# A hand-written state-space stage: who stores u, in which order it lies in memory, and where the modulation products stand

## The reference, cut to what matters

```python
shift, scale, gate = _modulation(c, a_mod_w, a_mod_b, 3)      # silu(c) @ w + b
h = _rms(x, a_norm_g) * (1.0 + scale) + shift                 # x: 1024 tokens x 1024
u, z = jnp.split(h @ w_in, 2, axis=-1)                        # each 1024 x 1024
ug = u.reshape(bsz, L, N_GROUPS, GROUP)                       # 64 groups of 16 channels
bu_r = jnp.einsum('blgc,gpc->blgp', ug, bb_r)                 # and bu_i
_, _, s_r, s_i = lax.associative_scan(_cplx_combine, (a_r, a_i, bu_r, bu_i), axis=1)
y = (jnp.einsum('blgp,gcp->blgc', s_r, C_re) - jnp.einsum('blgp,gcp->blgc', s_i, C_im))
y = gelu(y.reshape(bsz, L, 1024) + D * u)
# then glu, times silu(z), times w_out, gate, residual; four more such modulations in later stages
```

## Time and profile before

| | us |
|---|---|
| median of three runs | 4381.43 |
| profiled execution, its own time | 4385.33 |
| its span | 4383.5 |
| TensorE busy in the span | 4061.4 (93%) |
| VectorE / ScalarE / GpSimd busy | 2700.2 / 1218.4 / 382.8 |

### The profile page before, as it was taken

How to read it: one execution, slowest core, us unless ns; L and a number is a source line. 1 busy time by engine, 2 the same in 40 slices (tenths; PEclk the granted TensorE clock), 3 DMA queues, 4 the chain that set the end, 5 groups by cost and what they waited for, 6 DMA issues and landing times. The chain is left out here.

```text
span 4383.5 us, 74028 instructions
## 1 busy us (share of the span) xinstructions
PE 4061.4 (93%) x29536; PEld 2617.4 (60%) x29536; DVE 2700.2 (62%) x5234; ACT 1218.4 (28%) x2794; POOL 382.8 (9%) x313
## 2 busy tenths in 40 slices
PE   7969999999998999998799999989989995899998
PEld 4434856888666788665444444448847774444443
DVE  6427334433576544755777887854436555899997
ACT  2111222212575322833211111122125642222112
POOL 0100000000121000000211111110000000212221
PEclk8989999999999999998899999999989997999999
DMA  7697211132431212105777777750153104799997
GB/s 285 235 192 270 83 72 40 66 109 86 155 117 59 85 53 91 48 31 199 273 263 293 284 273 271 271 196 20 52 179 87 21 31 164 277 353 348 349 349 288
DMA packets 138205, 757.96 MB, mean 173 GB/s; under 512 B 14848, under 2 KB 53504, under 8 KB 102512
## 3 DMA queue, kind: packets, MB, share of 16 engines
q1 hardware_dynamic: 108048, 670.05, 41.1%
q0 software_dynamic: 24880, 65.29, 5.7%
q10 hardware_dynamic: 5040, 19.37, 1.3%
HBM read 663.98 MB, written 91.19 MB: 172 GB/s over the span
## 5 line engine op out<-in xcount | busy, mean ns | idle before, releaser
L442 PE MATMUL psum<-w_ring,arena 128*128 128x256 f32 (+1 forms) x2784 | 611.3, 378 | 19.1 <-PEq L202 8.3
L442 PEld LDWEIGHTS psum<-w_ring,arena 128*128 128x128 f32 x2784 | 523.1, 192 | 90.9 <-issue 20.5
L3442 PE MATMUL psum<-arena 128*64 128x512 f32 x2048 | 454.7, 596 | 6.6 <-ACT arena L3631 4.5
L3464 PE MATMUL psum<-arena 128*64 128x256 f32 x3472 | 381.5, 380 | 0.0
L442 PE MATMUL psum<-arena,w_ring 128*128 128x256 f32 x1600 | 354.6, 381 | 6.4 <-DVE arena L497 3.5
L3442 PE MATMUL psum<-w_ring,arena 128*64 128x512 f32 x1536 | 344.3, 597 | 5.2 <-ACT arena L3764 5.2
L442 PEld LDWEIGHTS psum<-arena,w_ring 128*128 128x128 f32 x1600 | 303.0, 191 | 50.1 <-DVE w_ring L538 3.6
L3464 PEld LDWEIGHTS psum<-arena 128*64 128x64 f32 x3472 | 246.6, 137 | 122.9
L3442 PEld LDWEIGHTS psum<-arena 128*64 128x64 f32 x2048 | 147.5, 137 | 281.4 <-issue 280.4
L1863 PE MATMUL psum<-arena 48*128 48x512 f32 (+5 forms) x1440 | 292.4, 517 | 8.8 <-PEq L1476 3.5
L508 DVE TENSOR_TENSOR arena<-arena,psum 128x256 f32<-128x256 f32 (+1 forms) x92 | 38.5, 418 | 386.2 <-PE psum L442 386.1
(11 more groups left out here) (464 smaller groups left out, 6006.9 us busy)
## 6 DMA issues: line engine op xcount, KB each, us to landing
w_ring<-in_wstream SPq DMA_DIRECT2D x162, 2048.0 KB, 9.3
arena<-in_wstream SPq DMA_DIRECT2D x97, 2048.0 KB, 7.8
x_rows<-arena SPq DMA_DIRECT2D x26, 512.0 KB, 2.8
w_ring<-in_wstream ACTq DMA_DIRECT2D x6, 2048.0 KB, 8.0
arena<-x_rows SPq DMA_DIRECT2D x18, 512.0 KB, 7.1
xn_rows<-arena POOLq DMA_DIRECT2D x18, 512.0 KB, 7.2
arena<-f_rows SPq DMA_DIRECT2D x8, 1024.0 KB, 7.7
arena<-in_x_first SPq DMA_DIRECT2D x4, 1024.0 KB, 25.0
```

The lines of the kernel that those rows point to most:

```text
L442: last = self.cr.nc.tensor.matmul(out, l, r, start=(start and k == 0), stop=(k == len(pairs) - 1), skip_group_check=True)
L3442: last = nc.tensor.matmul(cr.bank[bank][HT * h:HT * (h + 1), :], left[:, k], right[:, 4 * h + k, :], start=(start and k == 0), stop=(k == ...
L3464: last = nc.tensor.matmul(cr.bank[bank][HT * h:HT * (h + 1), 0:QW], left[:, k], right[:, k, QW * h:QW * (h + 1)], start=(start and k == 0) ...
```

## The change

1. `u_T` in DRAM is laid out as [8 positions, 16 channels, 64 groups, 128 chunks]. Transfer t of the U load is then one run of 32 KB for each of 16 partitions, where it was 64 pieces of 512 B for each.
2. ScalarE stores u itself, on its own DMA queue: after the copy of u product p it waits for that copy and issues eight transfers, each from 16 partitions, four pieces of 512 B from each. GpSimd stores only z. The semaphores `ut` count these transfers in the place of `st`.
3. The scan inputs stand after products 18 and 19 (they stood after 20 and 21), and the sixteen modulation products are spaced by a table: none after 18, two after 26. The slots change with them: tile `W_AIN + 3` comes earlier in slot 1, and m = 2 to 7 all use slot 2. SyncE's extra load that waits for product 23 stands before the load that follows m = 6 (it stood before the one that follows m = 7).

```diff
-FIRST_SLOTS.update({W_MOD1 + n: 1 if n % 2 else 2 for n in range(6)})
-FIRST_SLOTS.update({W_AIN + 3: 1})
-FIRST_SLOTS.update({W_MOD1 + n: 0 if n > 8 and n % 2 else 2 for n in range(6, N_MOD1)})
+FIRST_SLOTS.update({W_MOD1: 2, W_MOD1 + 1: 1, W_AIN + 3: 1})
+FIRST_SLOTS.update({W_MOD1 + n: 0 if n >= 8 and n % 2 == 0 else 2 for n in range(2, N_MOD1)})
...
-    uT, zT = cr.dram("u_T", [D, SEQ]), cr.dram("z_T", [D, SEQ])
+    uT, zT = cr.dram("u_T", [T_CH, GRP, GROUPS, NCH]), cr.dram("z_T", [D, SEQ])
...
-    K_AT, G_AT, IN_AT = 8, 12, 20
-    mods_after = lambda p: range(p - 16, p - 15 if p < 30 else N_MOD1) if 16 <= p < 31 else ()
+    K_AT, G_AT, IN_AT = 8, 12, 18
+    MODS_AFTER = {16: (0,), 17: (1,), 19: (2,), 20: (3,), 21: (4,), 22: (5,), 23: (6,), 24: (7,), 25: (8,), 26: (9, 10), 27: (11,), 28: (12,), 29: (13,), 30: (14, 15)}
...
+    def emptied(eng, u):
+        if u < 16:
+            eng.wait_ge(ut[u % 2], 128 * (u // 2))
+        elif u == 16:
+            eng.wait_ge(ut[1], 128 * 8)
+        else:
+            eng.wait_ge(st[1], 16 * (u - 16))
...
             for s in range(2):
-                sp.wait_ge(st[s], 16 * NU // 4)
+                sp.wait_ge(ut[s], 128 * 8)
             sp.wait_ge(s_gt, 16)
             for t in range(T_CH):
-                sp.dma_start(U[GRP * t:GRP * (t + 1)], uT.rearrange("(g c) t -> c g t", c=GRP)[:, :, t * NCH:(t + 1) * NCH]).then_inc(u_in, 16)
+                sp.dma_start(U[GRP * t:GRP * (t + 1)], uT[t]).then_inc(u_in, 16)
...
             for n in range(N_MOD1):
-                if n == 7:
+                if n == 6:
                     sp.wait_ge(un.full, 24)
                     cr.load_w(sp, cr.next_tile(W_AIN + 2))
...
                 pool.wait_ge(un.empty, u + 1)
-                pool.dma_start(dst, staged(u)).then_inc(stores_of(u), 16)
+                if m >= KT:
+                    pool.dma_start(zT[(m - KT) * P:(m - KT + 1) * P, h * 512:(h + 1) * 512], staged(u)).then_inc(st[1], 16)
...
                 nc.scalar.activation(staged(u), un.bank(u), ACT.Copy if u < NU // 2 else ACT.Silu).then_inc(un.empty, 1)
+                if u < 16:
+                    act.wait_ge(un.empty, u + 1)
+                    m, h = 4 * (u // 8) + u % 4, u // 4 % 2
+                    for g in range(8):
+                        act.dma_start(uT[4 * h:4 * h + 4, :, 8 * m + g, :].rearrange("t c n -> c t n"),
+                                      stage[GRP * g:GRP * (g + 1), u % 2].rearrange("c (t n) -> c t n", t=4)).then_inc(ut[u % 2], 16)
```

More of the change, by code:

```diff
@@ L574, in block_first @@
     st, s_kd, m_in = (st0, st1), (s_kd0, s_kd1), (m0, m1)
-    uT, zT = cr.dram("u_T", [D, SEQ]), cr.dram("z_T", [D, SEQ])
+    uT, zT = cr.dram("u_T", [T_CH, GRP, GROUPS, NCH]), cr.dram("z_T", [D, SEQ])
+    ut = cr.sems("first", "u_stored0 u_stored1")
     Kd = cr.dram("k_lags", [GRP, GROUPS, 2 * P])
@@ L615, in block_first @@
     row_bank, psM = (2, 6, 6), (cr.bank[3][:, 0:48], cr.bank[7][:, 0:84], cr.bank[7][:, 84:168])
-    K_AT, G_AT, IN_AT = 8, 12, 20
-    mods_after = lambda p: range(p - 16, p - 15 if p < 30 else N_MOD1) if 16 <= p < 31 else ()
+    K_AT, G_AT, IN_AT = 8, 12, 18
+    MODS_AFTER = {16: (0,), 17: (1,), 19: (2,), 20: (3,), 21: (4,), 22: (5,), 23: (6,), 24: (7,), 25: (8,), 26: (9, 10), 27: (11,), 28: (12,), 29: (13,), 30: (14, 15)}
+    mods_after = lambda p: MODS_AFTER.get(p, ())
     inputs_after = lambda p: range(half * (p - IN_AT), half * (p - IN_AT + 1)) if IN_AT <= p < IN_AT + 2 else ()
     staged = lambda u: stage[:, u % 2 if u < 16 else 1]
-    stores_of = lambda u: st[u % 2 if u < 16 else 1]
+    def emptied(eng, u):
[5 more added lines that the diff above has]
+            eng.wait_ge(st[1], 16 * (u - 16))
     with nc.Block(no_gpsimd_drain=True) as block:
@@ L683, in _ @@
                 m, h = 4 * (u // 8) + u % 4, u // 4 % 2
-                dst = (uT if m < KT else zT)[(m % KT) * P:(m % KT + 1) * P, h * 512:(h + 1) * 512]
                 pool.wait_ge(un.empty, u + 1)
-                pool.dma_start(dst, staged(u)).then_inc(stores_of(u), 16)
+                if m >= KT:
+                    pool.dma_start(zT[(m - KT) * P:(m - KT + 1) * P, h * 512:(h + 1) * 512], staged(u)).then_inc(st[1], 16)
                 i = u - K_AT - 1
@@ L695, in _ @@
                 pool.wait_ge(s_kd[k], 32 * 4)
-            pool.wait_ge(st[0], 16 * 8)
-            pool.wait_ge(st[1], 16 * (NU - 8))
+            pool.wait_ge(st[1], 16 * (NU - 16))
         @block.tensor
@@ L892, in _ @@
                 if u >= 2:
-                    act.wait_ge(stores_of(u), 16 * (u // 2 if u < 16 else u - 8))
+                    emptied(act, u)
                 nc.scalar.activation(staged(u), un.bank(u), ACT.Copy if u < NU // 2 else ACT.Silu).then_inc(un.empty, 1)
+                if u < 16:
[4 more added lines that the diff above has]
+                                      stage[GRP * g:GRP * (g + 1), u % 2].rearrange("c (t n) -> c t n", t=4)).then_inc(ut[u % 2], 16)
                 if u == 7:
@@ L902, in _ @@
                                          cr.bank[j % 2][:, 0:2 * P].rearrange("p (r n) -> p r n", r=2), ACT.Copy).then_inc(b_empty, 1)
-                if u == 23:
+                if u == 24:
                     row_1(0)
@@ L1086, in add_times @@
                 return tt(dst[:, 1], dst[:, 1], t1[:, 1], ALU.add)
-            dve.wait_ge(st[0], 16 * 8)
+            dve.wait_ge(ut[0], 128 * 8)
             ln(nc.vector.memset(step, 0.0))
```

## The result

The changed kernel takes 4393.13 us (median of 7 runs, 4390.82 to 4398.17). The kernel before took 4381.43 us (median of 7 runs, 4374.39 to 4385.89). The ratio is 1.0029 with a 95% interval of [1.002, 1.0038], so the change costs 11.7 us. The prediction was 4390 us, slower.

A forecast was written before the change was run, and what follows sets the result against it. TensorE is busy nearly throughout, so its 35.00 us idle after product 18, awaiting U and the tile behind it, counts. Terms +6.3 +2.8 +1.3 -2 +1 +5.4 -5.3 made +9.5, taken as 9 on 4381.4: 4390 us, range 4365 to 4401.

The forecast's parts named there:

- The path: Through the stage: product 15, its store, the U load, then the tile of m = 2 behind it; VectorE not on it.
- tiles beside the stores: Products 4 to 7: ScalarE's stores run beside weight tiles TensorE waits for; four steps at 0.7, 2.8 us later.
- the turns ahead of product 15: Turns of products 12 to 14: ScalarE's eight issues delay the copy TensorE's third transpose waits for; 6.3 us later.
- the last store: Product 15's u store, eight small transfers beside a weight tile: 10.5 us where it took 9.2, so +1.3.
- the U load: Load of U in 32 KB runs, still 16 partitions a transfer: 46 us, 2 us less for fewer packets.
- the z stores: Before the scan inputs, ScalarE's copy of product 18 waits for z stores, mostly inside the U wait; 1 us added.
- restart to the end of m = 8, z hold apart: From TensorE's restart after U: waits for tiles sharing slot 2 and 7 us before m = 7; 5.4 us longer.
- the tile of m = 2 no longer holds TensorE: After product 18 the scan inputs need U alone, not the tile that came 5.3 us after U; 5.3 us saved.
- end of m = 8: Sum of the terms where modulation product m = 8 ends: 378.7 us, 9.4 us later than 369.30; +9.5 by the path.
- the 82 GB/s of my row: Rate read from the old profile while U flowed to 16 partitions in 512 B pieces; gave the U load's 54 us bound.
- the rival that I gave 0.14: At the scan inputs: z stores wait for most of U's load, scan inputs start 7 us late, 4397 us; chance 0.14.
- the likeliest case: The forecast itself for the whole kernel: 4390 us, its own range 4383 to 4398; chance 0.52.

The follow-up runs named there:

- e11: Changed kernel with GpSimd instead of ScalarE issuing the eight small stores of each u product; 4385.47 us (one run).
- e7b: Changed kernel with ScalarE copying the scan inputs of products 18 and 19 ahead of that product's copy; 4387.88 us, ratio to before 1.0018.
- e3: Changed kernel with u_T padded in DRAM, so its eight U transfers to 16 partitions have 512 B pieces again; 4402.51 us (one run).
- e4b: Changed kernel with ScalarE issuing the u stores of products 12 to 15 after the copies of the turned G; 4380.85 us, ratio to before 0.9998.
- e1: Changed kernel with U loaded by one transfer to all 128 partitions in 32 KB runs; 4374.03 us, ratio to before 0.998.
- e5: Kernel before with the respacing alone, u stored and loaded as before; 4385.76 us, ratio to before 1.0.
- e8b: Changed kernel with the first 16 k_lags loads issued after m = 10 instead of m = 5; 4392.67 us, ratio to before 1.0025.
- e9: Changed kernel with one wide U load, turns first, scan input copies first and k_lags late, all together; 4351.99 us, ratio to before 0.9935.
- the four small edits: On the changed kernel: one wide U load, u stores after the turns, scan inputs copied first, k_lags loads late; together 4351.99 us.

## Why the prediction was right

The forecast was 9 us slower, and 11.7 were measured. The path held, and the sum came out near by luck, because errors of both signs stood in it. Term by term, in us, from the profile after:

| term | predicted | measured |
|---|---|---|
| tiles beside the stores | +2.8 | +2.0 |
| the turns ahead of product 15 | +6.3 | +11.4 |
| the last store | +1.3 | +0.5 |
| the U load | -2 | -9.1 |
| the z stores | +1 | +6.0 |
| restart to the end of m = 8, z hold apart | +5.4 | +7.3 |
| the tile of m = 2 no longer holds TensorE | -5.3 | -5.3 |
| end of m = 8 | +9.5 | +12.8 |

- **Tiles.** Product 12 was copied at 186.73, 2.0 us later than in the earlier trace rows. It was not four steps at 0.7, as I had it, but one wait of 3.44 us and the slow instruction behind it. In e11, where GpSimd issues the same transfers, no wait there is over 1.48 us and none has a slow instruction behind it.
- **Turns.** The mechanism and the size of the waits were right: 2.15, 2.16 and 2.70 more than the 0.25 of before, 7.0 together, for 6.3. What I left out was the clock (0.84 and 0.77 above). After such a wait the product ran for 8.26 or 9.04 us in the place of 7.03, and the turn for 1.60 or 1.97 in the place of 1.15: 4.5 us more. The size of this part is that of one execution: in e7b, with waits of 3.43, 2.45 and 2.96 us and no slow product, product 15 is copied at 228.21, 10.0 us later than before and close to the 227.3 of my sum. I had seen this price at the long wait (3.64 for 1.92 us) and did not put it on short ones. In e3 all three products were slow (8.72, 7.65 and 8.73 us). e4b takes all of it back: U is issued 11.7 us earlier.
- **The last store** took 9.66 us (231.60 to 241.26).
- **U.** I took 46 us, and it was 39.2: this term was mis-sized by 7 us. The reason for the small gain was right, and e1 to e3 show it. What I underrated is that the piece length has a price of its own on top, 5 to 7 us at either width. Some 2 of the 9.1 us are the slow load of the profile before (48.3 us, where e5 took 46.0). The estimate from the Trainium skill's figure (some 40 us) was the better one; the 82 GB/s of my row were measured on short pieces and so held both costs.
- **z stores.** Here the rival that I gave 0.14 came true beside the likeliest case. It said that the second z store would start only when most of U is in and that the scan inputs would start 7 us late. ScalarE's copy of product 18 ended its wait at 286.6, and the first lot took 16.4 us for 9.1. In e7b, without the hold, it took 10.4, so 6.0 us are the hold and 1.3 the slow clock behind the wait for U (0.86 granted from 277 to 287 us there). The row against it was a store beside a weight tile's packets, but those go to 128 partitions and are quick. A z store has 80 packets, five an engine; at 4.6 us for each packet of U ahead of one, that is 23 us (an estimate), and from its issue to its landing it took 23.8. Beside the 1.24 us packets of e1 one took 8.3 us, where the same sum gives 6.2. The rule that I cited, each engine going round its queues packet by packet (the Trainium skill, DMA: Bandwidth & Descriptors, Queues, rings and completion order), agrees with that number if each 32 KB packet of the profile is one packet in its sense, which no run here shows; I had drawn the wrong sum from it. It doesn't account for the 13.6 us or so beside packets of 512 B in e3.
- **The respacing** came out nearly as worked: from the restart to the end of m = 8 101.6 us passed, of which 6.0 are the z hold; 95.6 remain, for 93.7. The waits for the tiles of m = 4 to 6 were 1.03, 0.61 and 1.30 us, 0.9 more than my 2.0, and the instructions behind the wait at m = 7 ran slower than those behind the 2.90 us before. The wait at m = 7 was 7.15 for 7, and e8b shows that the k_lags loads ahead of the tile make it.

The wrong size of U (-7) was made up for by the turns (+5), the z stores (+5) and the respacing (+2). The sign stood on the right ground, ScalarE's issues ahead of the turns: e4b, in which ScalarE does not stand in TensorE's way, is level with before.

The profiled executions differ by only 6.9 us in their spans, while the stage ends 11.8 us later. The stretch behind the stage has the same work in both and spreads by that much between executions; the medians, +11.7, agree with the stage.

## What to carry to other kernels

A DMA issue is work of the engine that issues it: eight of them on ScalarE between a product's copy and the copies TensorE waits for cost more than the layout that they served brought in. When a load is slow, ask first how many partitions each transfer reaches; here one transfer to 128 partitions was worth 27 us of the load where the long pieces were worth 7, and the change left that undone. No run tried one wide load from the old layout, so it is not shown that the new one was needed for it. And measure each repair against the kernel that it repairs: against the changed kernel the four small edits gave some 20, 14, 7 and 2 us by their ratios to before, 43 in sum, and together they gave 41. Against before three of them looked like nothing or a loss.

## What the hardware showed that I had not expected

- A 32 KB packet took 4.6 us when all DMA engines wrote into 16 partitions, and 1.24 us when they wrote into 128.
- Another queue's 256 KB store took 23.8 us from issue to landing beside the former, 8.3 beside the latter (e1), and 2.3 in e9 (median of its six z stores up to 300 us). Beside packets of 512 B to 16 partitions it took 13.6 in e3 and 17.5 before (medians of two).
- Eight issues in a row took ScalarE 3.91 to 3.99 us at products 12 to 15 of the changed kernel (3.65 to 6.07 at the others), GpSimd mostly 4.03, and SyncE 3.67 us; so mostly 0.46 to 0.50 us each, whoever makes them. The eight loads of U in pieces of 512 B kept SyncE for 28.7 to 31.1 us.
- Waits of 2.4 to 3 us were followed by a slower TensorE in some cases and not in others: the product behind the turn took 8.26 us after 2.40, 7.03 after 2.41, and 9.04 after 2.95; in e7b it took 7.03 after 3.43, after 2.45 and after 2.96.
